# Block compression in a hybrid decoder step: units of 32 cache pages become units of 48, and the landing ring becomes five batches of four pages

## The reference, cut to what matters

```python
def nsa_compress(k, pe, phi1, phi2):
    B, L, G, d = k.shape
    nc = L // NSA_BLOCK
    kb = k[:, :nc * NSA_BLOCK].reshape(B, nc, NSA_BLOCK, G, d) + pe[None, None, :, None, :]
    kb = kb.transpose(0, 1, 3, 2, 4).reshape(B, nc, G, NSA_BLOCK * d)
    return jax.nn.silu(kb @ phi1) @ phi2
```

## Time and profile before

| | us |
|---|---|
| Time of the kernel, median of 3 runs | 2996.16 (2993.09 to 3001.28) |
| The profiled execution's own time | 2976.68 |
| Its span | 2974.9 |
| TensorE busy with matmuls | 2526.7 (85%) |
| VectorE busy | 1267.3 (43%) |
| ScalarE busy | 874.8 (29%) |
| The compression stage | about 1639 to 1951 of the span |
| Its 16 units of cache pages | 1668.01 to 1948.77 |

### The profile page before, as it was taken

How to read it: one execution, slowest core, us unless ns; L and a number is a source line. 1 busy time by engine, 2 the same in 40 slices (tenths; PEclk the granted TensorE clock), 3 DMA queues, 4 the chain that set the end, 5 groups by cost and what they waited for, 6 DMA issues and landing times. The chain is left out here.

```text
span 2974.9 us, 76189 instructions
## 1 busy us (share of the span) xinstructions
PE 2526.7 (85%) x28824; PEld 1635.2 (55%) x28824; DVE 1267.3 (43%) x3366; ACT 874.8 (29%) x2098; POOL 141.9 (5%) x233
## 2 busy tenths in 40 slices
PE   6999888899996359989999766569999997888878
PEld 4556455566664344445555755556676664555534
DVE  2121355545553832111110444435656654666633
ACT  1111344433332210010100000036766774444400
POOL 0000000011110100000000000000000001122100
PEclk9999999999998669989999778889999998998989
DMA  4000200077764332151104677630000004776732
GB/s 181 24 15 13 70 1 1 24 228 224 233 205 105 38 116 80 54 222 48 38 31 125 205 236 246 198 144 2 2 2 2 2 2 143 218 223 216 230 115 76
DMA packets 312632, 322.60 MB, mean 108 GB/s; under 512 B 72283, under 2 KB 289547, under 8 KB 311820
## 3 DMA queue, kind: packets, MB, share of 16 engines
q1 hardware_dynamic: 225116, 233.99, 25.2%
q10 hardware_dynamic: 87152, 83.73, 9.2%
HBM read 290.57 MB, written 30.27 MB: 108 GB/s over the span
## 5 line engine op out<-in xcount | busy, mean ns | idle before, releaser
L2198 PE MATMUL bank<-cm_room 64*64 64x64 f32 x8192 | 168.3, 248 | 111.5 <-issue 111.4
L2021 PE MATMUL bank<-cm_room 128*128 128x512 f32 (+3 forms) x576 | 226.9, 555 | 0.0
L2198 PEld LDWEIGHTS bank<-cm_room 64*64 64x64 f32 x8192 | 157.9, 161 | 121.1 <-issue 121.0
L2585 ACT ACTIVATE np_pT<-bank 128x512 f32<-128x512 f32 (+3 forms) x384 | 164.0, 461 | 134.1 <-PE bank L2505 134.1
L2519 PEld LDWEIGHTS bank<-kv,np_pT 128*64 128x64 f32 x4224 | 143.8, 137 | 104.4 <-ACT np_pT L2585 87.7
L2289 DVE COPY cm_room<-cm_room 128x1024 f32<-128x1024 f32 x128 | 126.7, 1053 | 160.4 <-DMA cm_room<-cache_nsa_kv 107.3
L2576 ACT ACTIVATE np_p<-np_p,np_nmax 128x640 f32<-128x640 f32 (+7 forms) x256 | 187.5, 732 | 0.3 <-DVE np_nmax L2637 0.3
L313 PE MATMUL bank<-ev_hT,ev_w 128*128 128x384 f32 (+1 forms) x576 | 176.4, 466 | 6.1 <-ACT zaT L256 6.1
L2519 PE MATMUL bank<-kv,np_pT 128*64 128x64 f32 x4224 | 179.2, 228 | 0.1
L2505 PE MATMUL bank<-ident,np_p 128*128 128x128 f32 x1056 | 171.8, 286 | 2.8 <-ACT np_pcT L2596 1.0
L2021 PEld LDWEIGHTS bank<-cm_room 128*128 128x128 f32 (+1 forms) x576 | 104.6, 183 | 118.5 <-issue 107.6
(11 more groups left out here) (514 smaller groups left out, 3793.8 us busy)
## 6 DMA issues: line engine op xcount, KB each, us to landing
ms_pg<-cache_mla SPq DMA_DIRECT2D x388, 144.0 KB, 2.6
ns_pg<-cache_nsa_kv SPq DMA_DIRECT2D x320, 128.0 KB, 2.6
cm_room<-cache_nsa_kv ACTq DMA_DIRECT2D x268, 128.0 KB, 3.3
cm_room<-cache_nsa_kv SPq DMA_DIRECT2D x244, 128.0 KB, 3.4
ns_pg<-cache_nsa_kv ACTq DMA_DIRECT2D x192, 128.0 KB, 3.0
ms_pg<-cache_mla ACTq DMA_DIRECT2D x124, 144.0 KB, 3.4
ev_w<-w_in_even SPq DMA_DIRECT2D x8, 768.0 KB
cm_room<-w_in_odd SPq DMA_DIRECT2D x24, 256.0 KB, 6.9
```

What stands on the lines that cost most here:

```text
L2021: t = nc.tensor.matmul(bank[:n, f, 0:hi - lo], hT[:, i // 3 % 2, k, at:at + n], wt[:, k, lo:hi], start=k == 0, stop=k == KD - 1)
L2198: t = nc.tensor.matmul(out(blk)[kind * HD:(kind + 1) * HD], phi[blk * BLK:(blk + 1) * BLK, kind, x, :], rows(kind, blk, x), start=x == 0, ...
L2585: nc.scalar.activation(pT[:, g % NPT, :(hi - lo) * P], bank[:, f, :(hi - lo) * P], ACT.Copy).then_inc(S["evA"], 1)
```

## The change

- A unit is 48 pages (`UP` = 48). The 512 pages make ten units of 48 and one of 32, so a unit can hold the end of one sequence and the beginning of the next. Lists worked out ahead say where units and sequences meet: `segments` (unit, sequence, place in the unit, page, count), `ends`, `done`, `last`.
- A batch is 4 pages (`BP` = 4) and the ring holds five of them (`NLAND` = 5), 20 pages in place of 48. A full unit has 12 batches.
- `silu(n)` does one activation for each segment. `products` and `evacuate` are called when a sequence's last unit has been passed, not at every second unit.
- ACT's loads ahead of `silu(n)` are the odd ones of batches `batches[n] + 5` to `batches[n + 1] + 4`, for full units 12n + 5 to 12n + 16.
- `hid` lies in columns of `kv` that are no longer needed, and the sample rows' buffer `tk` lies in the shared room.

```diff
@@ odd_projection
-        tk = sb("op_tk", [NS, 6 * KVW])
+        tk = place(6 * KVW)[:NS]
...
-UP = 32
-BP = 8
-NLAND = 6
+UP = 48
+BP = 4
+NLAND = 5
...
@@ compress
-    NU = CP // UP
-    NB = UP // BP
+    NU = -(-CP // UP)
+    sizes = [min(UP, CP - n * UP) for n in range(NU)]
+    batches = [0]
+    for size in sizes:
+        batches.append(batches[-1] + size // BP)
+    segments = []
+    for n, size in enumerate(sizes):
+        at = n * UP
+        while at < n * UP + size:
+            b = at // NPAGE
+            to = min((b + 1) * NPAGE, n * UP + size)
+            segments.append((n, b, at - n * UP, at - b * NPAGE, to - at))
+            at = to
+    ends = {b: max(i for i, x in enumerate(segments) if x[1] == b) + 1 for b in range(DB)}
+    done = {n: max(i for i, x in enumerate(segments) if x[0] == n) + 1 for n in range(NU)}
+    last = {b: max(x[0] for x in segments if x[1] == b) for b in range(DB)}
...
-        hid = sb("cm_hid", [P, 2, 2, NG, NPAGE])
+        hid = kv[:, 0:2, 0:2 * KVW].rearrange("p b (h g j) -> p b h g j", h=2, g=NG)
...
             @block.scalar
                 def silu(n):
-                    b, half = divmod(n, 2)
                     act.wait_ge(S["acc"], n + 1)
-                    if b >= 2:
-                        act.wait_ge(S["out"], b - 1)
-                    nc.scalar.activation(hid[:, b % 2, :, :, half * UP:(half + 1) * UP], ...
+                    for _, b, at, page, count in [x for x in segments if x[0] == n]:
+                        if b >= 2:
+                            act.wait_ge(S["out"], b - 1)
+                        nc.scalar.activation(hid[:, b % 2, :, :, page:page + count], ...
...
                 for n in range(NU):
-                    for m in range(NB * n + NLAND + 1, min(NB * (n + 1) + NLAND + 1, NU * NB), 2):
-                        load(act, AC, m)
+                    for m in range(batches[n] + NLAND, min(batches[n + 1] + NLAND, batches[NU])):
+                        if m % 2 == 1:
+                            load(act, AC, m)
                     silu(n)
...
             @block.tensor
+                ready = 0
                 for n in range(NU):
-                    pe.wait_ge(S["flat"], NB * (n + 1))
+                    pe.wait_ge(S["flat"], batches[n + 1])
                     if n >= 2:
-                        pe.wait_ge(S["hid"], n - 1)
+                        pe.wait_ge(S["hid"], done[n - 2])
                     hidden(...)
-                    if n >= 2 and n % 2 == 0:
-                        products(n // 2 - 1)
+                    while last[ready] < n:
+                        products(ready)
+                        ready += 1
...
             @block.vector
+                ready = 0
                 for n in range(2, NU):
                     flatten(n)
-                    if n >= 4 and n % 2 == 0:
-                        evacuate(n // 2 - 2)
-                evacuate(DB - 2)
-                evacuate(DB - 1)
+                    while last[ready] < n - 2:
+                        evacuate(ready)
+                        ready += 1
+                while ready < DB:
+                    evacuate(ready)
+                    ready += 1
```

More of the change, by code:

```diff
@@ L1877, in odd_projection @@
         early["soon"] = soon
-        tk = sb("op_tk", [NS, 6 * KVW])
+        tk = place(6 * KVW)[:NS]
+        assert at <= ROOM_EL
         s_x = [cleared(nc, ctx, f"op_s_x{k}") for k in range(NX)]
@@ L2129 @@
 PW = 2 * KVW
-UP = 32
-BP = 8
-NLAND = 6
+UP = 48
+BP = 4
+NLAND = 5
 CP = DB * NPAGE
-ROOM_EL = PHI_EL + NLAND * BP * PW + 2 * UP * PW + 512
+ROOM_EL = PHI_EL + NLAND * BP * PW + 2 * UP * PW
 def phi_room(early):
@@ L2204, in _ @@
             def _(sp):
-                for m in range(0, NU * NB, 2):
+                for m in range(0, batches[NU], 2):
                     load(sp, SP, m)
@@ L2210, in silu @@
                 def silu(n):
-                    b, half = divmod(n, 2)
                     act.wait_ge(S["acc"], n + 1)
-                    if b >= 2:
-                        act.wait_ge(S["out"], b - 1)
-                    nc.scalar.activation(hid[:, b % 2, :, :, half * UP:(half + 1) * UP], bank[:, 2 * (n % 2):2 * (n % 2) + 2, 0:2 * UP].rearrange("p h (g j) -> p h g j", g=NG),
-                                         ACT.Silu, bias=bias[:]).then_inc(S["hid"], 1)
+                    for _, b, at, page, count in [x for x in segments if x[0] == n]:
+                        if b >= 2:
+                            act.wait_ge(S["out"], b - 1)
+                        nc.scalar.activation(hid[:, b % 2, :, :, page:page + count],
+                                             bank[:, 2 * (n % 2):2 * (n % 2) + 2, 0:2 * sizes[n]].rearrange("p h (g j) -> p h g j", g=NG)[:, :, :, at:at + count],
+                                             ACT.Silu, bias=bias[:]).then_inc(S["hid"], 1)
                 for m in range(1, NLAND, 2):
@@ L2251, in products @@
                 def products(b):
-                    pe.wait_ge(S["hid"], 2 * b + 2)
+                    pe.wait_ge(S["hid"], ends[b])
                     if b == 0:
@@ L2267, in products @@
                     t.then_inc(S["out"], 1)
+                ready = 0
                 for n in range(NU):
-                    pe.wait_ge(S["flat"], NB * (n + 1))
+                    pe.wait_ge(S["flat"], batches[n + 1])
                     if n >= 2:
-                        pe.wait_ge(S["hid"], n - 1)
-                    hidden(lambda blk: bank[:, 2 * (n % 2) + blk, 0:2 * UP],
-                           lambda kind, blk, x: flat[blk * BLK:(blk + 1) * BLK, n % 2, kind, x].rearrange("p g j -> p (g j)")).then_inc(S["acc"], 1)
-                    if n >= 2 and n % 2 == 0:
-                        products(n // 2 - 1)
+                        pe.wait_ge(S["hid"], done[n - 2])
+                    hidden(lambda blk: bank[:, 2 * (n % 2) + blk, 0:2 * sizes[n]].rearrange("p (g j) -> p g j", g=NG),
+                           lambda kind, blk, x: flat[blk * BLK:(blk + 1) * BLK, n % 2, kind, x, :, 0:sizes[n]]).then_inc(S["acc"], 1)
+                    while last[ready] < n:
+                        products(ready)
+                        ready += 1
                 products(DB - 1)
@@ L2284, in flatten @@
                         dve.wait_ge(S["acc"], n - 1)
-                    for m in range(NB * n, NB * (n + 1)):
+                    for m in range(batches[n], batches[n + 1]):
                         dve.wait_ge(s_page[m % NLAND], 16 * BP * (m // NLAND + 1))
-                        at = m % NB * BP
+                        at = (m - batches[n]) * BP
                         for kind in range(2):
```

## The result

The changed kernel takes 3070.99 us (median of 4 runs, 3068.17 to 3072.32), the kernel before 2994.62 us in the runs beside it: a ratio of 1.026, with a 95% interval of 1.0232 to 1.0287. It is slower, by 76 us. The forecast was 3101 us with a range of 3045 to 3165: right in its sign and inside its range, and 30 us too high.

A forecast was written before the change was run, and what follows sets the result against it. Instruction refills bound TensorE's units before; the change adds waits for pages. Stage: 179.7 (units) + 199.6 (heads) + 7.2 + 1 (products) = 387.5 us against 282.0, +105, so 3101 us; range 3045 to 3165.

The forecast's parts named there:

- Units cost refills, not columns: TensorE's units: each costs four instruction refills, 17.6 us on average before, whatever its columns; larger units buy fewer refills.
- my ends of 2.10 and 3.15: TensorE's run of 128 at full clock: 2.10 us if columns don't matter, 3.15 if they alone matter.
- Four odd batches behind the SiLU: ACT's queue: four odd batches of the next unit wait behind `silu(n)`, so TensorE waits at each unit's head; decides the sign.
- The size of a head: TensorE's wait ahead of a full unit: 4 x 3.57 + 3.4 + 1.1 = 18.8 us; all heads 199.6 us.
- The size of a unit: TensorE's products: 16.5 us for a full unit, 14.7 for the last, 179.7 us for all eleven.
- part 3: Order of second products: copies and products ahead of four units cost 7.2 us; the last two sequences' products add 1 us.
- code ahead: Rival, chance 0.10: TensorE's refills go on while it waits; units of about 12.6 us, 39 us less, 3062.
- the half clock throughout a unit: Rival, chance 0.13: TensorE's clock stays at half for whole units, full ones 22.2 us; +57 us more, 3158.
- Products behind `evacuate`: For b = 1, 2, 4, 5, DVE's copies and second products delay TensorE's next unit: 4 x 1.8 = 7.2 us.
- The other sign: Rival, chance 0.05: ACT's odd batches are issued while TensorE works, so loads don't hold it up; stage perhaps 235, time 2949.
- From the profiled execution to the median: Whole kernel: the runs' median lies 19.5 us above the profiled execution, with the same stage addition; 3082 becomes 3101 us.

The follow-up runs named there:

- the lighter set-up: The kernel before with the bounds check of page numbers left out of the register set-up of page loads: 2992.57 us, ratio 1.0045 (1.0027 to 1.0062).

## Why the prediction was right, point by point

- **Units cost refills, not columns.** Right without loads: units of 64 and of 96 columns take the same 15 us. In the changed kernel it no longer holds. There TensorE is busy for 144.3 us in its eleven units and waits 20.0 us for "issue", so what a unit costs behind its head is mostly its runs, where columns count: a run of 128 with 96 columns took 2.87 us at full clock, between my ends of 2.10 and 3.15.
- **Four odd batches behind the SiLU.** Right, and it decides the sign: moving them turned 1.026 into 0.987. The dosage agrees: two batches 9.4 to 9.8 us, four 18.8, and four lighter ones 16.0. The 24.4 us of five batches fit too, but there the ring of 12 pages also holds up the queues.
- **The size of a head.** Predicted 18.8, measured 18.8. That it agrees so closely is luck, since its terms make up for each other: a batch 3.32 us and not 3.57, the landing of the last 4.2 us from the end of its issue to the copy (1677.71 to 1681.88) and not 3.4. For two batches the sum is too high by 2 us: 9.84 less 2 x 3.32 and 1.1 leaves 2.1 for the landing. All eleven heads: 197.8 us against 199.6.
- **The size of a unit.** This term was off. I took 16.5 us for a full unit and 14.7 for the last. Nine periods from 1698.67 to 2008.32 are 34.4 us each, so 15.5 us without their heads of 18.9 on average; the last period is 22.2 us, 12.4 without its 9.84. Together with part 3 I had 187.9 us outside the heads, and it was 366.2 - 197.8 = 168.4. What was too dear in it is the refills: I let three runs each take 3.66 us. In the first unit 378 records, nearly three runs, go without a pause in 10.76 us behind the head, and then only 0.41 and 1.15 us are waited for. The clock was priced about right: 0.50 for 3.46 us, then 0.92 on average over 12.17, so about 3.46 + 0.16 x 12.17 = 5.4 us at half. The DMA rate over the stage, 176 GB/s, was nearer 160 than 225, as said. The rival of "code ahead" was half right: much of a unit is there at once behind a wait, but at half clock first, so a unit isn't down at 12.6 us. That of the half clock throughout a unit was wrong.
- **Products behind `evacuate`.** The place was right: exactly the four heads of b = 1, 2, 4 and 5 are released by `evacuate`. The price was about right, 1.7 us and not 1.8: at unit 4 DVE's last copy of the unit is done at 1819.5, its copies of the result hold TensorE until 1820.31 (0.8 us, counted in the head), and TensorE goes from the first product to the unit in 0.87 us (1820.31 to 1821.18).
- **The other sign.** Its mechanism was real, though not in this kernel: with loads in time I had 235 us for the stage and 2949 us, and the kernel that does it takes 244 us and 2950. The agreement of the times to 1 us is luck, as the stage was 9 us longer than that sum.
- **From the profiled execution to the median.** I carried 19.5 us over to the runs. In the profiled executions the difference is 91.5 us, in the medians 76.4. Before's runs spread over 29 us (2972 to 3001), the changed kernel's over 4. Why before varies more is open.

The sum for the stage was +105 us and it was +84. Sorted by the terms of the prediction, with the 0.8 us of copies taken out of four heads: the units are 14.8 us cheaper than priced, the heads 5.0, part 3 with the last products 1.5. So the term that was mis-sized is the unit, priced from refills that TensorE had mostly got over during its wait. The time was off by 30 us and not by 21. The medians differ by 15 us less than the profiled executions do, and the 7 us outside the stage, which I had put at nothing, go the other way.

## What to carry to other kernels

When a ring of landing buffers becomes smaller than a unit of work, look at every queue that fills it and at what stands ahead of the fill in program order. If an engine both loads and waits for the unit's result, loads behind that wait can't overlap with the unit. In this loop the ring's depth against the unit's size says how many stand there: with twelve batches to a unit and a ring of five it is seven, with four eight, both with four of ACT; with a ring that holds a unit and more, as before, none. Count the batches behind the wait: each costs a full set-up and issue. And a gain that is real in a kernel without loads (here 71 us) can be had only with the supply in order; without that the same larger units came with a stage 84 us longer.

## What the runs showed of the hardware

- TensorE runs 128 products and then pauses, at a pace that is slower beside other DMAs. With page loads taken away, a unit of four runs went from 17.6 to 14.9 us (282.0 to 237.7 over 16); the granted clock was 0.84 with loads and 0.96 without, and its share in this wasn't separated.
- After waits of 17 to 20 us TensorE ran 160 to 378 records of 96 columns (the units from 1958.62 and from 1683.04) before its first "issue" pause, so more than one run is held ready during a wait.
- In the one profiled execution of the kernel before with cheaper issue, the stage was longer, 293.5 us against 282.0, with "issue" pauses up to 4.7 us and 117.9 us in all, where before had 3.6 and 111.4:

```profile
PE bank L2199 <- issue: 117.9, 58, 4.7
```

A possible reading is that pages then come in denser bursts and the refills wait behind them. It isn't shown: the profiled execution of before was itself 18 us under the median of 2994.62, the kernel before with ACT's loads ahead had a stage of 283.2 us, and over all runs the lighter set-up costs 0.45%.
- The price of columns at full clock: 2.87 us for a run of 128 records with 96 columns, 2.10 with 64, and 39 ns a record at half clock (3.46 us for 88). None of it showed in the time of a unit as long as refills were slower, as in the two kernels without loads.
